# Opening of a transformer kernel: input scale folded into the pool weights, modulation blocks reordered, pool products placed among the running sums

## Chip, core and metric

The kernel runs on one core of a Trainium2 chip. The metric is the device time of one execution in microseconds (us), median of several runs. The engines of the core are named as the profile names them: PE is TensorE (matrix multiply; PEld is its weight load), DVE is VectorE, ACT is ScalarE, POOL is GpSimd, SP is SyncE, which here only issues transfers. All work runs once; each engine has its own instruction stream, and the streams meet at semaphores.

## The reference, cut to the opening

The whole kernel is one pooling layer with a feed-forward part, then two further layers (attention, chunked recurrence, gated spatial mixing). The change touches only the pooling layer, of which this is computed (1024 tokens, 1024 channels, float32):

```
mod = silu(c) @ mod_w + mod_b                      # 6 x 1024 numbers
sh1, sc1, g1, sh2, sc2, g2 = split(mod, 6)
hx = x * (1 + sc1) + sh1
for each group g of 256 channels, window w = 2, 4, 8, 16:
    d = mean of hx over a window of w tokens - hx  # shift cancels in d
    ox = (d @ pool_w[g]) * pool_scale
x = layer_norm(ALPHA * x + g1 * ox, ln_g0, ln_b0)
x = layer_norm(ALPHA * x + g2 * swiglu(x * (1 + sc2) + sh2, ...), ...)
```

## The kernel before

Channels lie on the 128 partitions, so `x` is 8 tiles `resid[:, k, :]` of 128 channels by 1024 tokens, and the layer norm's sums over channels are products with a tile of ones. The layer norm works on two halves of the tokens, `e = 0` and `e = 1`. "Tile 3" or "block 3" below counts from 0.

**Transfers.** SP issues the parameters, the first half of `x`, then the 12 blocks of `mod_w` (2 MB each, three buffers, so a block waits for `mod_mm` of the block three before it), with the second half of `x` ahead of block 2, and then the first weight slabs of the feed-forward part. ACT issues `pw` (the pool weights, 1 MB) and after it `edge` (16 KB, correction factors at the ends of the windows).

**Modulation.** `mod_block(n)` on PE multiplies block n by `silu_c`; `mod_read(n)` on ACT copies the row to `mod_row`; `mod_columns(n)` on PE turns it into 4 columns. Two blocks make one of the six vectors; before, the blocks come in the order shift, scale, gate.

**Pool.** On ACT, `pad(k)` copies tile k into one of three padded buffers `xpad` and `scale_x(k)` multiplies `resid` by ALPHA. On DVE, a running sum over tile k takes 1 to 4 additions (L1814), two small edge corrections (L1823, L1825) and one operation that writes `acc` (L1827). When all 8 are done, DVE forms the scale `sc1p` and `pool_gain` (L1833 to L1838) and passes twice over each tile of `acc` (L1841: scale and add shift; L1842: subtract shift). Then PE computes output tile j from two tiles of `acc` (L812, 4 matmuls), DVE adds it to `resid` (L1868), and PE sums the result for the mean (`mean_part`, L692).

**First norm and projection.** Mean to all partitions (`spread_mean`, L724), subtraction on DVE (`center`, L1877), squares on ACT (L1360), their sums on PE (`square_part`, L692), `root` on ACT (L1364), `reciprocal` on DVE (L1881), `spread_rstd` on PE (L724), then `gain` on DVE (L1888), `tmp` and `h_hi` on ACT (L1427, L1406), and `h_lo` on DVE for even k (L1895), on POOL for odd k (L500). `project_first` (L624 to L626) needs `h_lo` of tile k for its step k, which is 6 matmuls; between the steps of half 0 it sums squares of half 1.

The order on each engine is the order in which the code is written; no scheduler changes it.

Of the kernel before, what the change touches and what calls it, by code (L numbers as in the profile page):

```python
# [24 lines left out]
ALU = mybir.AluOpType  # L25
# [3 lines left out]
P = 128  # L29
# [107 lines left out]
def build(nc, x_t, params, mod_w, pool_w, w_in, w_c, edges, w_spatial, b_spatial, out):  # L137
    with ExitStack() as ctx:
# [73 lines left out]
        MOD_HALF = MOD_BLOCKS // 2  # L212
# [90 lines left out]
        mod_bank = BANK[6]  # L303

# [16 lines left out]
        par_ld, small_ld = beat("par_ld", 16), beat("small_ld", 32)  # L321
# [60 lines left out]
        def _(sp):  # L382
# [11 lines left out]
            for n in range(MOD_BLOCKS):  # L394
                if n >= MOD_BUFFERS:
                    sp.wait_ge(mod_mm.sem, mod_mm.at(n - MOD_BUFFERS))
                if n in X_BEFORE:
                    half = X_BEFORE.index(n)
                    tiles = slice(half * KT // 2, (half + 1) * KT // 2)
                    sp.dma_start(resid[:, tiles, :], x_t[:, tiles, :]).then_inc(x_ld[half].sem, 16)  # L400
                sp.dma_start(mod_big[n % MOD_BUFFERS][:], mod_w[n]).then_inc(mod_ld[n % MOD_BUFFERS].sem, 16)
# [215 lines left out]
        def _(pe):  # L617
# [158 lines left out]
            def mod_columns(n):  # L776

                pe.wait_ge(mod_out.sem, mod_out.at(n))
                for j in range(HALF // P):
                    col = HALF + n * (HALF // P) + j  # L780
                    mm = pe.matmul(PS[1][:, col:col + 1], mod_row[n % 2][:, j * P:(j + 1) * P], ones[:, 0:1], start=True, stop=True,
                                   skip_group_check=True)
                mm.then_inc(mod_turn.sem, 1)

            def mod_part(n):
                mod_block(n)
                if n not in (0, MOD_HALF):
                    mod_columns(n - 1)

            pe.wait_ge(const.sem, 14)  # L790
            pe.wait_ge(siluc.sem, 1)
            pe.wait_ge(dve_first.sem, 1)
            for n in range(MOD_HALF):
                mod_part(n)
            mod_columns(MOD_HALF - 1)

            pe.wait_ge(dve_first.sem, 6)
            pe.matmul(PS[0][:, 0:3], ones[:], lam_prod[:], start=True, stop=True).then_inc(lam_mm.sem, 1)

            pe.wait_ge(small_ld.sem, small_ld.at(0))  # L800
            pe.wait_ge(lam_x.sem, lam_x.at(0))
            pe.wait_ge(mod_col.sem, 1)
            mod_after = {1: 7, 3: 8, 6: 9}
            mod_part(6)
            for j in range(KT):
                g, e = j // 2, j % 2
                pe.wait_ge(p_done.sem, 2 * g + 2)
                if j >= 2:
                    pe.wait_ge(z_done.sem, j - 1)
                for t0 in (0, HALF):  # L810
                    for k in range(2):
                        mm = pe.matmul(pool_bank[e][:, t0:t0 + HALF], pw[:, g, k, e * P:(e + 1) * P],  # L812
                                       acc[:, 2 * g + k, t0:t0 + HALF], start=(k == 0), stop=(k == 1),
                                       skip_group_check=True)
                mm.then_inc(pool_mm.sem, 1)
                if j in mod_after:
                    mod_part(mod_after[j])
                if j >= 1:
                    pe.wait_ge(z_done.sem, j)
                    for half in range(2):  # L820
                        mean_part(0, half, j - 1)

            pe.wait_ge(z_done.sem, KT)
            for e in range(2):
                mean_part(0, e, KT - 1)
# [7 lines left out]
            pe.wait_ge(mod_col.sem, 3)  # L833
# [476 lines left out]
        def _(act):  # L1310
# [27 lines left out]

            act.wait_ge(const.sem, 14)
# [4 lines left out]
            reads = {3: 0, 4: 1, 5: 2, 6: 3, 7: 4}  # L1344
            for k in range(3, KT):
                mod_read(reads[k])
                pad(k)
                scale_x(k)
            mod_read(MOD_HALF - 1)
            act.wait_ge(lam_mm.sem, 1)  # L1350
            act.activation(shift_mean[:], PS[0][:, 2:3], ACT.Identity, scale=1.0 / D, bias=eps[:, 0:1]).then_inc(lam_x.sem, 1)
            act.activation(lam_exp[:], PS[0][:, 0:2], ACT.Exp).then_inc(lam_x.sem, 1)
            for n in range(MOD_HALF, 10):
                mod_read(n)

# [54 lines left out]
            for n in range(KT + 1):  # L1410
                square_centred(0, n)
            mod_read(10)
            root(0, 0)
            for n in range(KT + 1, KT + 4):
                square_centred(0, n)
            mod_read(11)
            act.wait_ge(mod_col.sem, 3)
            for n in range(2 * KT):
                e, k = divmod(n, KT)
                if n in (1, 2, 3, 4):  # L1420
                    square_centred(0, KT + 3 + n)
# [356 lines left out]
        def _(dve):  # L1778
# [24 lines left out]
            dve.wait_ge(small_ld.sem, 32)  # L1803
            for k in range(KT):
# [25 lines left out]
            dve.wait_ge(p_diff.sem, p_diff.at(KT - 1))  # L1830
            dve.wait_ge(mod_turn.sem, mod_turn.at(MOD_HALF - 1))
            nb = COL["mod_b"]
            dve.tensor_tensor(mod[:, 0:24], PS[1][:, HALF:HALF + 24], par[:, nb:nb + 24], ALU.add).then_inc(mod_col.sem, 1)  # L1833
            dve.wait_ge(mod_col.sem, 1)
            dve.tensor_scalar(sc1p[:], mod[:, SC1], 1.0, None, ALU.add).then_inc(px_step.sem, 1)
            step[0] += 1
            dve.wait_ge(px_step.sem, step[0])
            chained(dve.tensor_tensor(pool_gain[:], mod[:, G1], par[:, COL["pool_scale"]:COL["pool_scale"] + KT], ALU.mult))  # L1838

            for k in range(KT):  # L1840
# [3 lines left out]
            def modulation_part(first, blocks):  # L1844

                dve.wait_ge(mod_turn.sem, mod_turn.at(blocks - 1))
                cols, columns = slice(first, 4 * blocks), slice(HALF + first, HALF + 4 * blocks)
                dve.tensor_tensor(mod[:, cols], PS[1][:, columns], par[:, nb + first:nb + 4 * blocks], ALU.add).then_inc(mod_col.sem, 1)

            def modulation_rest():  # L1850

                modulation_part(24, 10)
                dve.wait_ge(mod_col.sem, 2)
                chained(dve.tensor_scalar(sc2p[:], mod[:, SC2], 1.0, None, ALU.add))
                chained(dve.tensor_tensor(ffn_b0[:], ln_b0, sc2p[:], ALU.mult))
                dve.tensor_tensor(ffn_b0[:], ffn_b0[:], mod[:, SH2], ALU.add).then_inc(mod_col.sem, 1)


            ln_b0 = par[:, COL["ln_b0"]:COL["ln_b0"] + KT]
            chained(dve.tensor_scalar(res_b0[:], ln_b0, ALPHA, None, ALU.mult))  # L1860
            chained(dve.tensor_scalar(da_gain[:], par_col("da_g"), 1.0 - LAM_INIT, None, ALU.mult))
            dve.wait_ge(lam_x.sem, lam_x.at(0))
            chained(dve.scalar_tensor_tensor(neg_lam[:], lam_exp[:, 1:2], LAM_INIT, lam_exp[:, 0:1], ALU.subtract, ALU.subtract))

            for j in range(KT):
# [3 lines left out]
                   .then_inc(z_done.sem, 1)  # L1869

# [29 lines left out]
            for n in range(KT, KT + 2):  # L1900
                center(0, n)
            modulation_rest()
            reciprocal(0, 0)
            for n in range(KT + 2, 2 * KT):
                center(0, n)
            for e in range(2):
                for k in range(KT):
                    gain(0, resid, k, e, "ln_g0", n_out)
                    if k % 2 == 1:
                        split_low(0, e * KT + k - 1)  # L1910
                if e == 0:
                    reciprocal(0, 1)
                    modulation_part(40, MOD_BLOCKS)
# [620 lines left out]
```

## Time and profile before

| | |
|---|---|
| median of 3 runs | 3077.92 us (3076.68 to 3078.0) |
| profiled execution, its own time | 3076.16 us |
| its span | 3074.4 us |
| PE busy | 2864.0 us (93%) |
| DVE, ACT, POOL busy | 1453.5, 774.6, 1212.1 us |
| mean granted TensorE clock | 0.97 |

Busy time says how much of the span an engine had an instruction at work. PE is the engine that is busy nearly throughout, so a wait of PE costs time wherever it lies, but the table does not say in which stage it waits; the rows below are of the first 143 us. In the page's line of 40 slices (each 77 us) the first slice of PE has the digit 5, the second 8, nearly all others 9.

### The profile page before, as it was taken

The numbers are of one execution on the slowest core, as the hardware profiler recorded it, in microseconds if no ns is written. First come the engines' busy times: TensorE is split into PE (matmuls) and PEld (weight loads), VectorE is DVE, ScalarE is ACT, GpSimd is POOL, SyncE is SP. The second block draws the span as 40 slices with busy tenths as digits, with TensorE's granted clock in tenths as the row PEclk, the third lists the DMA queues.
The fourth block names the chain that finished last, engine by engine and source line by source line (L and its number), as shares of the span: only waits on it lengthen the run. The fifth ranks groups of instructions, "written<-read, shape, count | busy, mean of one in ns | idle before, by whom it ended". The sixth has DMA issues, their size and how long they took to land.

```text
span 3074.4 us, 38842 instructions
## 1 busy us (share of the span) xinstructions
PE 2864.0 (93%) x14522; PEld 2285.2 (74%) x14522; DVE 1453.5 (47%) x2224; ACT 774.6 (25%) x1383; POOL 1212.1 (39%) x573
## 2 busy tenths in 40 slices
PE   5899999999988899999978998898879999999997
PEld 2578888888866677777756787787658878888885
DVE  7433343343374555565555574737350134444445
ACT  3420000000043333333331322222333331211212
POOL 0254444444343322222221333423254356566554
PEclk9999999999999999999998999999889999999999
DMA  9111111111111001011001111111222211111113
GB/s 370 63 55 48 48 48 48 48 48 48 41 49 69 22 29 33 27 34 34 27 28 28 34 50 41 55 34 48 83 96 89 89 69 69 55 55 68 55 62 117
DMA packets 58223, 185.27 MB, mean 60 GB/s; under 512 B 17300, under 2 KB 17428, under 8 KB 55976
## 3 DMA queue, kind: packets, MB, share of 16 engines
q1 hardware_dynamic: 37152, 152.68, 14.6%
q10 hardware_dynamic: 21000, 31.61, 2.9%
q8 instruction: 49, 0.80, 0.1%
q14 instruction: 22, 0.18, 0.0%
HBM read 163.22 MB, written 21.05 MB: 60 GB/s over the span
## 4 chain that ended last, share of the span: by engine, by line
PE 78%; DVE 11%; issue 4%; ACT 4%; POOL 1%; DMA 1%; DVEq 0%; ACTq 0%; POOLq 0%; SPq 0%
PE ps L624 24%; PE ps L626 23%; PE ps L625 23%; PE ps L954 2%; PE ps L761 1%; PE ps L692 1%; PE ps L965 1%; DVE acc L1932 1%; DVE tree L1814 1%; DVE stat L2081 1%; PE ps L812 1%; DVE da_p L2092 1%; DVE ml_t L2216 1%; DVE da_al L2101 1%; ACT ps L1590 1%
## 5 line engine op out<-in xcount | busy, mean ns | idle before, releaser
L484 POOL TENSOR_TENSOR slab_hi<-slab_raw,zero 128x1024 fp32r<-128x1024 f32 x227 | 442.4, 1949 | 1525.7 <-PE ps L626 1434.4
L624 PE MATMUL ps<-h_hi,slab_hi 128*128 128x512 f32 x2512 | 1001.6, 399 | 25.5 <-DVE h_lo L1895 10.9
L625 PE MATMUL ps<-h_lo,slab_hi 128*128 128x512 f32 x2512 | 988.1, 393 | 0.0
L626 PE MATMUL ps<-h_hi,slab_lo 128*128 128x512 f32 x2512 | 988.1, 393 | 0.0
L486 POOL TENSOR_TENSOR slab_lo<-slab_raw,slab_hi 128x1024 fp32r<-128x1024 f32 x227 | 574.2, 2530 | 17.8
L624 PEld LDWEIGHTS ps<-h_hi,slab_hi 128*128 128x128 f32 x2512 | 478.1, 190 | 137.2 <-issue 21.7
L626 PEld LDWEIGHTS ps<-h_hi,slab_lo 128*128 128x128 f32 x2512 | 477.0, 190 | 102.5
L625 PEld LDWEIGHTS ps<-h_lo,slab_hi 128*128 128x128 f32 x2512 | 478.4, 190 | 95.4
L1932 DVE TENSOR_TENSOR acc<-ps,acc 128x512 f32<-128x512 f32 x448 | 294.9, 686 | 57.5 <-PE ps L626 55.1
L1939 DVE TENSOR_TENSOR ffn_p<-ps,ffn_g 128x1024 f32<-128x1024 f32 x22 | 27.0, 1225 | 456.3 <-PE ps L626 449.1
L1930 DVE SCALAR_TENSOR_TENSOR resid<-ps,mod,resid 128x512 f32<-128x512 f32 x320 | 212.8, 742 | 0.0
L624 PE MATMUL ps<-ffn_hi,slab_hi 128*128 128x512 f32 x352 | 139.4, 396 | 1.4 <-issue 1.4
L625 PE MATMUL ps<-ffn_lo,slab_hi 128*128 128x512 f32 x352 | 138.7, 394 | 0.0
L626 PE MATMUL ps<-ffn_hi,slab_lo 128*128 128x512 f32 x352 | 138.7, 394 | 0.0
L1434 ACT ACTIVATE ffn_g<-ps 128x1024 f32<-128x1024 f32 x22 | 22.6, 1028 | 397.9 <-PE ps L626 397.9
L624 PE MATMUL ps<-sg_yh,slab_hi 128*128 128x512 f32 x256 | 103.8, 405 | 5.4 <-DVE acc L1932 3.4
L2101 DVE TENSOR_TENSOR da_al<-ps,da_ah 128x512 fp32r<-128x512 f32 (+2 forms) x96 | 53.2, 554 | 114.8 <-ACT da_ah L1526 114.7
L626 PE MATMUL ps<-sg_yh,slab_lo 128*128 128x512 f32 x256 | 101.0, 395 | 0.0
L625 PE MATMUL ps<-sg_yl,slab_hi 128*128 128x512 f32 x256 | 100.9, 394 | 0.0
L2081 DVE TENSOR_REDUCE stat<-ps 128x1 f32<-128x256 f32 (+7 forms) x128 | 90.8, 751 | 16.4 <-PE ps L954 15.8
L2356 DVE COPY sg_t<-ps 128x1024 f32<-128x1024 f32 x16 | 19.6, 1225 | 159.1 <-PE ps L761 159.0
L2375 DVE SCALAR_TENSOR_TENSOR sg_v<-ps,par,sg_b 128x1024 f32<-128x1024 f32 x16 | 20.5, 1284 | 150.4 <-PE ps L626 150.4
(315 smaller groups left out, 3847.1 us busy)
## 6 DMA issues: line engine op xcount, KB each, us to landing
slab_raw<-w_in SPq DMA_DIRECT2D x168, 512.0 KB, 3.5
mod_big<-mod_w SPq DMA_DIRECT2D x12, 2048.0 KB, 12.9
slab_raw<-w_c SPq DMA_DIRECT2D x43, 512.0 KB, 3.5
res_scr<-resid ACTq DMA_DIRECT2D x4, 2048.0 KB, 7.6
resid<-res_scr ACTq DMA_DIRECT2D x2, 4096.0 KB, 12.9
gv_scr<-sg_t ACTq DMA_DIRECT2D x16, 512.0 KB, 2.6
slab_raw<-gv_scr SPq DMA_DIRECT2D x16, 512.0 KB, 3.5
resid<-x_t SPq DMA_DIRECT2D x2, 2048.0 KB, 16.8
```

What stands on the lines that cost most here:

```text
L484: pool.tensor_tensor(hi, raw[slot][:], zeros, ALU.add).then_inc(hi_done.sem, 1)
L486: pool.tensor_tensor(wlo[slot][:].rearrange("p k f -> p (k f)"), raw[slot][:], hi.bitcast(F32), ALU.subtract).then_inc(done.sem, 1)
L624: pe.matmul(dst, w_h, r_h, start=first, stop=False, skip_group_check=True)
L625: pe.matmul(dst, w_h, r_l, start=False, stop=False, skip_group_check=True)
L626: return pe.matmul(dst, w_l, r_h, start=False, stop=last, skip_group_check=True)
L692: mm = pe.matmul(bank[32 * g:32 * g + 32, :], weights, tile[:, g * P:(g + 1) * P], start=(opens and k == 0), stop=(k == KT - 1), skip_grou ...
L761: mm = pe.transpose(dst[:, b * P:(b + 1) * P], src(b), ident[:])
L954: mm = pe.matmul(score_bank[c][:, t0:t1], q[rows, cols], k[rows, t0:t1], start=(n == 0 and not diagonal), stop=(n == 2), skip_group_check= ...
L1930: ins = dve.scalar_tensor_tensor(to[:, d, cols], src[:, cols], gain[:, d:d + 1], to[:, d, cols], ALU.mult, ALU.add)
L1932: ins = dve.tensor_tensor(to[:, d, cols], src[:, cols], to[:, d, cols], ALU.add)
L2081: dve.tensor_reduce(stat[:, 4 * (i % 2) + c:4 * (i % 2) + c + 1], PS[c][:, 0:n], AX_X, ALU.max, negate=True)\
L2101: dve.tensor_tensor(a_lo[:, slots, :], turn_bank[:, 0:blocks * P].rearrange("p (b q) -> p b q", q=P), a_hi[:, slots, :].bitcast(F32), ALU. ...
```

## The change

1. **Scale folded into the weights.** The two passes over `acc` (16 operations of 128x1024 on DVE) go. ACT multiplies the pool weights by `sc1p` instead (`scale_weights`, 8 operations of 128x256). The shift is not added and subtracted any more; for `sh1` DVE forms `mod[SH1] - mod[SH1]` and adds it to `ffn_b0`.
2. **Order of the modulation blocks** (`MOD_ORDER`): scale, gate, shift. The scale is read out after 2 blocks, the gate after 4, each into PSUM columns of its own.
3. **Interleaving.** DVE: running sums 0 to 3, scale, sums 4 to 6, gate, the additions to `resid` of tiles 0 and 1, sum 7, the other additions. PE: pool products from after block 1 on, blocks 2 to 9 between them, `mean_part` two tiles behind.
4. **Loads.** `edge` is issued first on ACT's queue; `pw` after the parameters have landed.
5. **Norm.** The Sqrt table is loaded by a dummy operation on `warm` before the mean; DVE subtracts the mean from 4 tiles of half 1 before the first `gain` (instead of 8) and from the other 4 between the gains; the last squares of half 1 move from steps 0 to 3 of `project_first` to steps 3 to 6, and `root(0, 1)` on ACT from before `tmp` 6 to before `tmp` 7. The small operations on the lambdas move to the start.

The core of the diff:

```diff
+        MOD_ORDER = (2, 3, 4, 5, 0, 1) + tuple(range(6, 12))
@@ PE
-            pe.wait_ge(mod_col.sem, 1)
-            mod_after = {1: 7, 3: 8, 6: 9}
-            mod_part(6)
-            for j in range(KT):
-                g, e = j // 2, j % 2
+            def pool_tile(j):
+
+                g, e = j // 2, j % 2
                 pe.wait_ge(p_done.sem, 2 * g + 2)
+                pe.wait_ge(p_diff.sem, p_diff.at(2 * g + 1))
                 if j >= 2:
                     pe.wait_ge(z_done.sem, j - 1)
...
+            mod_block(0)
+            mod_block(1)
+            mod_columns(0)
+            mod_columns(1)
+            pe.wait_ge(lam_x.sem, lam_x.at(0))
+            pool_tile(0)
+            mod_block(2)
+            mod_block(3)
+            mod_columns(2)
+            mod_columns(3)
+            pool_tile(1)
+            mod_block(4)
+            for j in range(2, KT):
+                pool_tile(j)
+                pool_means(j - 2)
+                if j < 7:
+                    mod_block(j + 3)
+                if j == 4:
+                    pe.wait_ge(mod_col.sem, 4)
+                if j < 7:
+                    mod_columns(j + 2)
+            pool_means(KT - 2)
+            pool_means(KT - 1)
             mod_columns(9)
...
             def first_squares(k):
-                if k < 4:
-                    square_part(0, 1, 4 + k)
+                if 3 <= k < 7:
+                    square_part(0, 1, 1 + k)
@@ ACT
-            act.dma_start(pw[:], pool_w).then_inc(small_ld.sem, 16)
             act.dma_start(edge[:], edges).then_inc(small_ld.sem, 16)
             act.wait_ge(par_ld.sem, 16)
+            act.dma_start(pw[:], pool_w).then_inc(par_ld.sem, 16)
...
+            def scale_weights(g):
+
+                act.wait_ge(par_ld.sem, 32)
+                act.wait_ge(mod_col.sem, 2)
+                for k in range(2):
+                    act.activation(pw[:, g, k, :], pw[:, g, k, :], ACT.Copy, scale=sc1p[:, 2 * g + k:2 * g + k + 1]).then_inc(p_done.sem, 1)
...
-                if n == 6:
+                if n == 7:
                     root(0, 1)
@@ DVE
-            for k in range(KT):
-                chained(dve.tensor_scalar(acc[:, k, :], acc[:, k, :], sc1p[:, k:k + 1], mod[:, k:k + 1], ALU.mult, ALU.add))
-                dve.tensor_scalar(acc[:, k, :], acc[:, k, :], mod[:, k:k + 1], None, ALU.subtract).then_inc(p_done.sem, 1)
...
+            for k in range(4):
+                window(k)
+            pool_scale()
+            for k in range(4, 7):
+                window(k)
+            pool_gate()
+            for j in range(2):
+                pool_add(j)
+            window(7)
+            for j in range(2, 5):
+                pool_add(j)
...
-            for n in range(KT + 2, 2 * KT):
+            for n in range(KT + 1, KT + 4):
                 center(0, n)
...
+                    if e == 0 and k in (1, 3):
+                        for n in range(2):
+                            center(0, KT + 3 + k + n)
```

On PE before, around the first pool products (L772 is `mod_block`, L781 `mod_columns`, L798 the lambda product, L812 the pool product; names are the program's):

```order
L781 MATMUL ps<-ones_62,mod_row1_94 128x1 [waits mod_out]
L781 MATMUL ps<-ones_62,mod_row1_94 128x1 x3
L798 MATMUL ps<-lam_prod_76,ones_62 128x3 [waits dve_first]
L772 MATMUL ps<-mod_big0_90,silu_c_70 1x512 [waits mod_ld0,mod_col,mod_out,lam_x,small_ld]
L772 MATMUL ps<-mod_big0_90,silu_c_70 1x512 x7
L812 MATMUL ps<-acc_60,pw_102 128x512 [waits p_done]
L812 MATMUL ps<-acc_60,pw_102 128x512 x3
```

And of the changed program, from the first pool product (L795) on:

```order
L795 MATMUL ps<-acc_60,pw_102 128x512 [waits p_diff,p_done,lam_x]
L795 MATMUL ps<-acc_60,pw_102 128x512 x3
L773 MATMUL ps<-mod_big2_92,silu_c_70 1x512 [waits mod_out,mod_ld2]
L773 MATMUL ps<-mod_big2_92,silu_c_70 1x512 x7
L773 MATMUL ps<-mod_big0_90,silu_c_70 1x512 [waits mod_out,mod_ld0]
...
L782 MATMUL ps<-ones_62,mod_row0_93 128x1 [waits mod_out]
...
L782 MATMUL ps<-ones_62,mod_row1_94 128x1 [waits mod_out]
...
L795 MATMUL ps<-acc_60,pw_102 128x512 [waits p_diff,p_done]
...
L773 MATMUL ps<-mod_big1_91,silu_c_70 1x512 [waits mod_out,mod_ld1]
...
L795 MATMUL ps<-acc_60,pw_102 128x512 [waits z_done,p_diff,p_done]
```

The pool products stood behind blocks 0 to 6; now product 0 stands ahead of block 2, and product 2 is the first that waits for DVE's addition (`z_done`).

On DVE before, from the end of running sum 7 to the first addition to `resid`:

```order
L1827 SCALAR_TENSOR_TENSOR acc_60<-tree3_101,xpad1_96 128x1024 [waits px_step]
L1833 TENSOR_TENSOR mod_69<-ps,par_68 128x24 [waits mod_turn,p_diff]
L1835 TENSOR_SCALAR sc1p_71<-mod_69 128x8 [waits mod_col]
L1838 TENSOR_TENSOR pool_gain_73<-mod_69,par_68 128x8 [waits px_step]
L1841 TENSOR_SCALAR acc_60<-acc_60,sc1p_71,mod_69 128x1024 [waits px_step]
L1842 TENSOR_SCALAR acc_60<-acc_60,mod_69 128x1024 [waits px_step]
...
L1868 SCALAR_TENSOR_TENSOR resid_89<-ps,pool_gain_73,resid_89 128x1024 [waits x_scaled,pool_mm,px_step]
```

And of the changed program, from the end of running sum 6 to the end of sum 7 (L1862 writes `acc`, L1898 adds to `resid`):

```order
L1862 SCALAR_TENSOR_TENSOR acc_60<-tree3_101,xpad0_95 128x1024 [waits px_step]
L1870 TENSOR_TENSOR mod_69<-ps,par_68 128x8 [waits mod_turn]
L1883 TENSOR_TENSOR pool_gain_73<-mod_69,par_68 128x8 [waits mod_col]
L1898 SCALAR_TENSOR_TENSOR resid_89<-ps,pool_gain_73,resid_89 128x1024 [waits x_scaled,pool_mm,px_step]
L1898 SCALAR_TENSOR_TENSOR resid_89<-ps,pool_gain_73,resid_89 128x1024 [waits x_scaled,pool_mm]
L1849 TENSOR_TENSOR tree0_98<-xpad1_96 128x1039 [waits p_diff,px]
...
L1862 SCALAR_TENSOR_TENSOR acc_60<-tree3_101,xpad1_96 128x1024 [waits px_step]
```

The two passes over `acc` are gone, and the first two additions stand ahead of the last running sum.

On ACT before, in half 0 of the projection, from `h_hi` 5 to `h_hi` 7 (L1427 is `tmp`, L1406 `h_hi`, L1364 the root of half 1):

```order
L1406 ACTIVATE h_hi_58<-tmp1_115 128x512 [waits s_tmp]
L1364 ACTIVATE std1_111<-ps,eps_67 128x128 [waits n_ssum]
L1427 ACTIVATE tmp2_116<-resid_89,ffn_b0_75,sc2p_72 128x512 [waits s_lo0,n_out]
L1406 ACTIVATE h_hi_58<-tmp2_116 128x512 [waits s_tmp]
L1427 ACTIVATE tmp3_117<-resid_89,ffn_b0_75,sc2p_72 128x512 [waits s_lo1,n_out]
L1406 ACTIVATE h_hi_58<-tmp3_117 128x512 [waits s_tmp]
```

And of the changed program, at the same place (L1455 is `tmp`, L1432 `h_hi`, L1386 a square, L1390 the root):

```order
L1432 ACTIVATE h_hi_58<-tmp1_115 128x512 [waits s_tmp]
L1386 ACTIVATE sq3_107<-resid_89 128x512 [waits n_ssum,n_cent]
L1455 ACTIVATE tmp2_116<-resid_89,ffn_b0_75,sc2p_72 128x512 [waits s_lo0,n_out]
L1432 ACTIVATE h_hi_58<-tmp2_116 128x512 [waits s_tmp]
L1390 ACTIVATE std1_111<-ps,eps_67 128x128 [waits n_ssum]
L1455 ACTIVATE tmp3_117<-resid_89,ffn_b0_75,sc2p_72 128x512 [waits s_lo1,n_out]
```

The last square of half 1 now stands right before `tmp` 6, and the root between `h_hi` 6 and `tmp` 7.

## Rows read from the trace of the kernel before

**Rows 1.** Chain that ended last, 0 to 143 us: start, us, what.

```profile
1.88 15.81 DMA edge<-edges
...
31.86 1.25 DVE tree L1814
...
49.76 1.25 DVE tree L1814
...
56.50 0.19 DVE mod L1833
...
69.81 1.29 DVE resid L1868
...
79.63 1.83 PE ps L772 x16
81.46 0.98 PE ps L781 x8
82.44 0.57 PE ps L692 x16
83.02 3.63 PE ps L812 x8
...
106.11 5.48 DVE resid L1877 x9
...
112.75 1.28 ACT L1364
114.05 0.38 ACT std L1364
114.45 0.95 DVE rstd L1881
...
134.31 0.81 ACT tmp L1427
...
137.20 0.50 PE ps L624
...
139.78 0.76 DVE resid L1888
```

**Rows 2.** Timeline of PE, opening: start, us, instruction, idle before and releaser.

```profile
21.29 3.59 PE L772 MATMUL ps<-mod_big,silu_c 128*1 128x512 f32 x16 [1.20 <-DMA mod_big<-mod_w]
24.81 1.87 PE L781 MATMUL ps<-ones,mod_row 128*128 128x1 f32 x8
31.08 3.59 PE L772 MATMUL ps<-mod_big,silu_c 128*1 128x512 f32 x16 [4.40 <-DMA mod_big<-mod_w]
...
56.89 3.38 PE L772 MATMUL ps<-mod_big,silu_c 128*1 128x512 f32 x16 [4.63 <-issue]
60.30 7.13 PE L812 MATMUL ps<-acc,pw 128*128 128x512 f32 x16
```

**Rows 3.** Timeline of ACT: first pads, the read of block 0, the root of half 1.

```profile
11.50 2.95 ACT L1332 ACTIVATE xpad<-resid 128x1024 f32<-128x1024 f32 x3 [7.65 <-DMA resid<-x_t]
...
20.15 0.60 ACT L1324 ACTIVATE mod_row<-ps 128x512 f32<-128x512 f32 x1 [2.86 <-PE ps L772]
...
132.67 0.37 ACT L1364 ACTIVATE std<-ps,eps 128x128 f32<-128x128 f32 x1 [2.60 <-PE ps L692]
```

**Rows 4.** Timeline of DVE: the first gain of half 0.

```profile
118.85 1.40 DVE L1888 SCALAR_TENSOR_TENSOR resid<-resid,par,ps 128x512 f32<-128x512 f32 x2
```

**Rows 5.** Timeline of PE: end of the means, and both starts of the projection.

```profile
103.45 0.64 PE L692 MATMUL ps<-resid,ones 128*32 128x128 f32 x16 [0.81 <-DVE resid L1868]
...
122.02 0.76 PE L624 MATMUL ps<-h_hi,slab_hi 128*128 128x512 f32 x1 [3.23 <-DVE h_lo L1895]
...
142.81 0.79 PE L624 MATMUL ps<-h_hi,slab_hi 128*128 128x512 f32 x1 [3.08 <-DVE h_lo L1895]
```

**Rows 6.** Stretch by engine in half 0 of the projection; PEclk is the granted clock.

```profile
122.00:128.50 6.50, 6.48 (x28) 4.00 (x28) 3.20 (x5) 6.37 (x11) 2.57 (x2) 0.52 0.01 3
```

**Rows 7.** Timeline of POOL: the first weight slab is split.

```profile
90.63 1.89 POOL L484 TENSOR_TENSOR slab_hi<-slab_raw,zero 128x1024 fp32r<-128x1024 f32 x1 [85.00 <-DMA slab_raw<-w_in]
```

More of the change, by code:

```diff
@@ L303, in build @@
         mod_bank = BANK[6]
+        mod_cols = [BANK[2][:, QUARTER:QUARTER + 48], BANK[7][:, QUARTER:QUARTER + 48]] + [BANK[3][:, 0:48]] * 4
         res_scr = nc.dram_tensor("res_scr", [P, KT, T], F32, kind="Internal").ap()
@@ L779, in mod_columns @@
                 for j in range(HALF // P):
-                    col = HALF + n * (HALF // P) + j
-                    mm = pe.matmul(PS[1][:, col:col + 1], mod_row[n % 2][:, j * P:(j + 1) * P], ones[:, 0:1], start=True, stop=True,
-                                   skip_group_check=True)
+                    col = MOD_ORDER[n] * (HALF // P) + j
+                    mm = pe.matmul(mod_cols[n // 2][:, col:col + 1], mod_row[n % 2][:, j * P:(j + 1) * P], ones[:, 0:1],
+                                   start=True, stop=True, skip_group_check=True)
                 mm.then_inc(mod_turn.sem, 1)
[L785 to L801, printed above, removed]
-            pe.wait_ge(mod_col.sem, 1)
-            mod_after = {1: 7, 3: 8, 6: 9}
-            mod_part(6)
-            for j in range(KT):
+            def pool_tile(j):
                 g, e = j // 2, j % 2
                 pe.wait_ge(p_done.sem, 2 * g + 2)
+                pe.wait_ge(p_diff.sem, p_diff.at(2 * g + 1))
                 if j >= 2:
@@ L815, in _, with pool_means @@
                 mm.then_inc(pool_mm.sem, 1)
[L816 to L825, printed above, removed]
+            def pool_means(j):
+                pe.wait_ge(z_done.sem, j + 1)
+                for half in range(2):
+                    mean_part(0, half, j)
+            pe.wait_ge(const.sem, 14)
+            pe.wait_ge(siluc.sem, 1)
+            pe.wait_ge(dve_first.sem, 6)
+            pe.matmul(PS[0][:, 0:3], ones[:], lam_prod[:], start=True, stop=True).then_inc(lam_mm.sem, 1)
+            mod_block(0)
[21 more added lines that the diff above has]
+            pool_means(KT - 1)
             mod_columns(9)
@@ L832, in _ @@
             mod_block(11)
-            pe.wait_ge(mod_col.sem, 3)
+            pe.wait_ge(mod_col.sem, 6)
             mod_columns(10)
@@ L1343, in _ @@
                 scale_x(k)
[L1344 to L1347, printed above, removed]
-                scale_x(k)
[L1349 to L1353, printed above, removed]
+            mod_read(0)
+            pad(3)
+            scale_x(3)
+            mod_read(1)
+            pad(4)
+            scale_weights(0)
+            pad(5)
+            for g in range(1, 4):
+                scale_weights(g)
+            pad(6)
+            for k in (4, 5):
+                scale_x(k)
+            mod_read(2)
+            pad(7)
+            scale_x(6)
+            mod_read(3)
+            scale_x(7)
+            for n in range(4, 10):
                 mod_read(n)
+            act.activation(warm[:], eps[:], ACT.Sqrt)
             def square(norm, n, src):
@@ L1836, in _, with modulation_part @@
[L1836 to L1840, printed above, removed]
-                chained(dve.tensor_scalar(acc[:, k, :], acc[:, k, :], sc1p[:, k:k + 1], mod[:, k:k + 1], ALU.mult, ALU.add))
-                dve.tensor_scalar(acc[:, k, :], acc[:, k, :], mod[:, k:k + 1], None, ALU.subtract).then_inc(p_done.sem, 1)
[L1844 to L1848, printed above, removed]
+            def modulation_part(turned, cols):
+                dve.wait_ge(mod_turn.sem, mod_turn.at(turned))
+                dve.tensor_tensor(mod[:, cols], mod_cols[turned // 2][:, cols], par[:, nb + cols.start:nb + cols.stop], ALU.add)\
+                   .then_inc(mod_col.sem, 1)
@@ L1853, in modulation_rest @@
-                dve.wait_ge(mod_col.sem, 2)
+                modulation_part(9, slice(SH2.start, SC2.stop))
+                dve.wait_ge(mod_col.sem, 5)
                 chained(dve.tensor_scalar(sc2p[:], mod[:, SC2], 1.0, None, ALU.add))
                 chained(dve.tensor_tensor(ffn_b0[:], ln_b0, sc2p[:], ALU.mult))
+                chained(dve.tensor_tensor(ffn_b0[:], ffn_b0[:], mod[:, SH1], ALU.add))
                 dve.tensor_tensor(ffn_b0[:], ffn_b0[:], mod[:, SH2], ALU.add).then_inc(mod_col.sem, 1)
-            ln_b0 = par[:, COL["ln_b0"]:COL["ln_b0"] + KT]
@@ L1860, in _, with pool_add @@
[L1860 to L1865, printed above, removed]
+            def pool_add(j):
                 dve.wait_ge(pool_mm.sem, j + 1)
@@ L1869, in _ @@
                    .then_inc(z_done.sem, 1)
+            for k in range(4):
[9 more added lines that the diff above has]
+                pool_add(j)
+            modulation_part(5, SH1)
+            dve.wait_ge(mod_col.sem, 4)
+            chained(dve.tensor_tensor(mod[:, SH1], mod[:, SH1], mod[:, SH1], ALU.subtract))
+            for j in range(5, KT):
+                pool_add(j)
             def center(norm, n):
@@ L1899, in _ @@
                 center(0, n)
-            for n in range(KT, KT + 2):
-                center(0, n)
             modulation_rest()
+            center(0, KT)
             reciprocal(0, 0)
-            for n in range(KT + 2, 2 * KT):
+            for n in range(KT + 1, KT + 4):
                 center(0, n)
```

44 lines of the change are left out of this document (28 added, 16 removed).

## Prediction

> **What bounds the kernel now.** I read the page first: PE is busy for 93% of the span, but only for about half of the first slice. So any time to be had or lost lies where PE waits, and the change lies wholly in the first 143 us. Next I followed the chain that ended last through that stretch [rows 1]. It begins with a transfer: DVE waits for `edge` until 17.7 us, though the first half of `x` was there at 11.50 [rows 3]. From there the chain is DVE alone, running sums until 56.5, small operations, then sixteen passes over `acc`, and at 69.81 the first addition to `resid`. Then it is PE, in a fixed rhythm: product 3.63 us, mean sums 0.57, and three times a modulation block (1.83) with its columns (0.98) [rows 1]. The means end at 103.45 + 0.64 = 104.09 [rows 5]. Then norm: subtraction from 106.11, table load and root, reciprocal, first gain at 118.85 [rows 4], first projection matmul at 122.02 [rows 5]. The reader is to see two engines taking turns: DVE runs while PE has almost nothing (a few blocks between waits for transfers, rows 2), and then PE runs while DVE waits. The change overlaps the turns.
>
> I time it by walking through the changed order with durations of the rows, in the clock of the profiled execution, up to the second projection half (gain 8, before at 139.78). Behind it order and work are the same on all engines, so a shift there goes to the end.
>
> **Up to the scale.** The modulation blocks come by the same transfers, so block 1 still runs at 21.29 and its columns follow. Columns 0 stood at 24.81 for 1.87 [rows 2]; the changed order puts columns 1 directly behind: 28.5 at that pace. DVE's sums 0 to 3 take 31.86 - 17.7 = 14.2 us [rows 1], so they are done by then if they start before 14.3. With `edge` ahead of `pw`, they start when `x` and its pads are there: 11.50 + 1 at the latest, though sum 3 needs `pad(3)`, which stands behind the read of block 0 (20.15, rows 3): 21.8 + 4.3 = 26.1. So the scale waits for PE, and is formed at 28.5 + 0.45 = 28.95. The folding costs ACT eight operations of 128x256. No row has that shape; 128x128 takes 0.37 and 128x512 0.60 [rows 3], and I take 0.4. Only the first two lie on a path (product 0 starts at 29.7); the others, 2.4 us, lie beside DVE's sums 4 to 6.
>
> **The anchor.** DVE goes on with sums 4 to 6. Sum 7 began at 49.76, so they take 49.76 - 31.86 = 17.9 [rows 1]: 46.85. Gate 0.4, one addition 1.3: 48.6. PE meanwhile does product 0, blocks 2 and 3 with their reads on ACT and their columns, product 1 and block 4. At the full clock that ends near 46, and if product 0 runs at half clock (3.3 us more) near 48.5. Product 2 waits for the first addition either way: 48.65. This is where PE stops waiting.
>
> **PE's run.** From there PE has, by the order, products 2 to 7, means 0 to 5, blocks 5 to 9 and columns 4 to 8 without a wait for anything late: 6 x 3.63 + 6 x 0.57 + 5 x 1.83 + 5 x 0.98 = 21.8 + 3.4 + 9.15 + 4.9 = 39.3, so 87.9. Each product needs an addition two back. DVE returns from sum 7 at about 56.5 (48.6 + 1.3 + 6.7), and product 4, the first to need that, comes at 62.7. Means 6 and 7 and the last addition: 89.35. Before it was 104.09, so the gain here is **14.75 us**. The transfers do not stop this: block 11 may be issued when block 8 is done, at 76, before at 81.9, so the weight slabs come no later than the 90.63 of [rows 7]; with four operations of about 2 us on POOL both are split by 99, and they are needed at 105.
>
> **Norm.** The subtraction starts at 91.35. Eight tiles at 0.61 (5.48 over 9, rows 1), five small operations (1.0) and one tile: 97.8. The root no longer has the table load of 1.28 in front [rows 1]; it follows the last of the squares at 97.9, and the reciprocal is done at 99.2. Now another wait ends last: PE still has block 11 and columns 10 ahead of the spread, 97.85 + 1.83 + 0.98 + 1.09 = 101.75. That is gain 0, against 118.85: the gain grows to **17.1**.
>
> **Given back.** Half 0 of the projection. Before, from gain 0 to gain 8 went 139.78 - 118.85 = 20.93. Now the square of the last tile is summed after step 6, and ACT's root stands ahead of `tmp` 7, so step 7 waits for step 6 through the root. Measured from gain 0: `h_lo` 6 is ready at 15.0 (pairs of tiles every 4.1 us while DVE puts subtractions between, then ACT's 1.9 us for each tile with a square), step 6 and the square end at 17.6, root 0.37, and from `tmp` 7 to the matmuls of step 7 took 137.20 - 134.31 = 2.89 [rows 1]. Step 7 starts at 20.85, behind an idle PE of 3.1 us. Before both starts of the projection PE had been idle for 3.08 and 3.23 us [rows 5], and the granted clock behind the latter was 0.52, which is 1.2 GHz [rows 6]; the same after 4.40 and 4.63 us [rows 2], where a block takes 3.59 or 3.38 instead of 1.83. So I take the lower level for step 7 (2.85, as from 122.02 to the second step) and the spread behind it (1.8): gain 8 at 25.5, and **4.6 us** of the 17.1 go.
>
> On this the Trainium skill ("TensorE: Matmul & The Clock Gate", Part 1, What's actually happening) says that the activity window runs freely, not in step with the kernel, so that the same gap may or may not lower the clock. By the row gaps of this size always did; by the page the outcome is open, and then the sum would be that of rival 1.
>
> **Sum.** 17.1 - 4.6 = 12.5. 3076.16 - 12.5 = 3063.7 for an execution like the profiled one; the median of the runs lay 1.8 above it, so **3065.4**.
>
> **Rivals.**
> 1. *Clock stays up across the 3.1 us gap* (chance 0.22). Step 7 takes 1.4 and the spread 0.9: gain 8 at 23.2, gain 14.8, **3063.1**. For it: 3.1 is at the edge of the gaps seen; against it: 3.08 lowered it too [rows 5].
> 2. *The scale is late* (0.10). If `edge` lands no earlier than before, the sums 0 to 3 end at 31.86 and everything up to the anchor is 3.3 later: **3068.7**. Against it: the 16 KB now go first in their queue. Nearby: the interleaved run has waits the sum does not have (an addition late for product 4, which has 62.7 - 57.8 = 5 us of slack).
> 3. *The gain is taken back later* (0.05): some later stage is bound by something that does not move, **3077**. Against it: behind gain 8 no row is bound by a transfer that was issued early; POOL's slabs have about 6 us of slack.
> 4. *Slower: PE runs the interleaved stretch at 1.2 GHz* (0.04). Products are now mixed with blocks whose one-column weights use PE little, and PE idles between 28.5 and 29.7 and perhaps before 48.65. Every us of the 39.3 at the lower level costs one more. The gain is gone once 12.5 of 39.3 run so; all of it is 3065.4 + 39 = **3104**. Against it: before, the same mix ran at 3.63 and 1.83 through 40 us [rows 1], and even the first two products behind a 4.63 us gap took 7.13 together, full pace [rows 2].
>
> **The numbers.** What is left, 0.59, goes to the forecast. Its own bounds: columns 1 at full clock (-0.9), product and block times as they are, the 128x256 operations between 0.2 and 0.6 (only two count, 0.4 each way), the projection at lower clock for longer or shorter (1.5 each way). That gives 3063 to 3068; with rivals 1 and 2 the range is **3061.5 to 3069.5**. A difference of 0.2% is 6.2 us, about what a measurement of this kernel can tell from none. Faster by more: forecast, rivals 1 and 2 except a small part, 0.90; within: 0.06; slower: 0.04.
>
> **What would show it.** In the changed profile: DVE's first running sum at 10 to 13 us instead of 17.7; no waits of DVE in sums 4 to 6; product 2 on PE at 48.65 released by DVE; no idle of PE from there to about 88; means done at 89 to 90; gain 0 near 101.8, released by PE's spread and not by the root; PE idle 3 us before step 7 of the projection; gain 8 at about 127.3 where it was at 139.78. The prediction would be wrong first if product 2 starts past 52, next if blocks take 3.4 instead of 1.8 in the interleaved run, and last if PE's wait before step 7 is not there (then the time is nearer 3061) or is much longer.

## The result and the profile after

The changed kernel takes 3058.54 us (median of 4 runs, 3055.9 to 3059.09) against 3077.3 us before (4 runs, 3075.4 to 3078.0). The ratio is 0.9938 with a 95% interval of 0.9921 to 0.9956, so it is faster by 0.4 to 0.8%. The forecast had the direction, but 12.5 us of gain where 18.8 were measured; the time lies 3 us under the stated range. The profiled spans differ by 3074.4 - 3056.8 = 17.6 us. A second comparison of the same program (`after_again` below) gave 0.995 (0.9936 to 0.9964), a gain of some 15 us by the ratio and 18.6 by the medians (3057.41 against 3076.01). So the runs place the gain at 15 to 19 us, and the two intervals reach from 11 to 24.

The timeline of PE after, from block 0 to the end of the means (start, us, instruction, idle before and releaser); it answers to [rows 2] and the first of [rows 5]:

```profile
15.97 3.59 PE L773 MATMUL ps<-mod_big,silu_c 128*1 128x512 f32 x16 [9.70 <-DMA mod_big<-mod_w]
20.94 3.59 PE L773 MATMUL ps<-mod_big,silu_c 128*1 128x512 f32 x16 [1.38 <-DMA mod_big<-mod_w]
24.46 2.24 PE L782 MATMUL ps<-ones,mod_row 128*128 128x1 f32 x16
28.21 5.37 PE L795 MATMUL ps<-acc,pw 128*128 128x512 f32 x8 [1.51 <-issue]
...
43.46 1.90 PE L773 MATMUL ps<-mod_big,silu_c 128*1 128x512 f32 x16
46.56 3.67 PE L795 MATMUL ps<-acc,pw 128*128 128x512 f32 x8 [1.20 <-DVE resid L1898]
...
53.37 3.68 PE L795 MATMUL ps<-acc,pw 128*128 128x512 f32 x8
...
85.68 0.64 PE L693 MATMUL ps<-resid,ones 128*32 128x128 f32 x16 [0.37 <-DVE resid L1898]
```

Product 2 (46.56) is the last one that DVE releases late. From there to the last mean PE has no wait longer than 0.37 us, and the means end at 86.32 instead of 104.09. The rhythm is 53.37 - 46.56 = 6.81 us for a product, the mean sums of a tile, a block and its columns.

DVE after, its sums and their waits, which answers to the first rows of [rows 1]:

```profile
10.48 1.24 DVE L1849 TENSOR_TENSOR tree<-xpad 128x1039 f32<-128x1039 f32 x1 [2.15 <-DMA edge<-edges]
...
21.21 1.24 DVE L1849 TENSOR_TENSOR tree<-xpad 128x1039 f32<-128x1039 f32 x1 [0.96 <-ACT xpad L1339]
...
26.74 0.17 DVE L1870 TENSOR_TENSOR mod<-ps,par 128x8 f32<-128x8 f32 x1 [1.36 <-PE ps L782]
...
27.02 1.24 DVE L1849 TENSOR_TENSOR tree<-xpad 128x1039 f32<-128x1039 f32 x1
...
45.13 2.48 DVE L1898 SCALAR_TENSOR_TENSOR resid<-ps,pool_gain,resid 128x1024 f32<-128x1024 f32 x2
...
98.34 1.41 DVE L1935 SCALAR_TENSOR_TENSOR resid<-resid,par,ps 128x512 f32<-128x512 f32 x2 [0.58 <-PE ps L725]
...
122.87 1.41 DVE L1935 SCALAR_TENSOR_TENSOR resid<-resid,par,ps 128x512 f32<-128x512 f32 x2 [5.30 <-PE ps L725]
```

The sums start at 10.48 instead of 17.7. The scale (26.74) waits for PE's columns. The first gain (98.34, before 118.85) is released by PE's spread, not by the root. Gain 8, the first of half 1, stands at 122.87, before at 139.78: 16.9 us of the 17.6 are there.

Half 0 of the projection ends with the wait that the change brought in. PE and ACT after:

```profile
119.32 0.50 PE L625 MATMUL ps<-h_hi,slab_hi 128*128 128x512 f32 x1 [3.19 <-POOL h_lo L501]
...
120.92 1.91 PE L725 MATMUL ps<-rstd,ident 128*128 128x128 f32 x8
125.91 0.80 PE L625 MATMUL ps<-h_hi,slab_hi 128*128 128x512 f32 x1 [3.08 <-DVE h_lo L1942]
```

```profile
116.20 0.37 ACT L1390 ACTIVATE std<-ps,eps 128x128 f32<-128x128 f32 x1 [3.58 <-PE ps L693]
```

Step 7 starts behind 3.19 us of idle PE. The root on ACT had waited 3.58 us for the square summed behind step 6, with `tmp` 7 queued behind it. The spread of the reciprocal then takes 1.91 us at a granted clock of 0.50; before, it was this row:

```profile
138.69 1.05 PE L724 MATMUL ps<-rstd,ident 128*128 128x128 f32 x8
```

### The profile page after: what moved, and what is told of

Read it like the earlier page. It is cut to its first block, busy times and chain, and to the rows that moved or that the text cites. A ratio compares the mean times of both kernels' runs of the same rounds, so it can differ in the third digit from the quotient of the medians.

```text
span 3056.8 us, 38843 instructions
## 1 busy us (share of the span) xinstructions
PE 2856.2 (93%) x14522; PEld 2283.4 (75%) x14522; DVE 1442.6 (47%) x2212; ACT 777.6 (25%) x1392; POOL 1212.0 (40%) x573
## 4 chain that ended last, share of the span: by engine, by line
PE 79%; DVE 10%; issue 4%; ACT 4%; DMA 1%; POOL 1%; DVEq 0%; ACTq 0%; SPq 0%; POOLq 0%
PE ps L625 24%; PE ps L627 23%; PE ps L626 23%; PE ps L961 2%; PE ps L762 1%; PE ps L693 1%; PE ps L972 1%; DVE acc L1981 1%; DVE stat L2130 1%; PE ps L795 1%; DMA mod_big<-mod_w 1%; DVE da_p L2141 1%; DVE ml_t L2265 1%; DVE da_al L2150 1%; PE ps L725 1%
## 5 line engine op out<-in xcount | busy, mean ns | idle before, releaser
L2130 DVE TENSOR_REDUCE stat<-ps 128x1 f32<-128x256 f32 (+7 forms) x128 | 90.8, 750 | 17.6 <-PE ps L961 16.9
```

What stands on the lines that cost most here:

```text
L2130: dve.tensor_reduce(stat[:, 4 * (i % 2) + c:4 * (i % 2) + c + 1], PS[c][:, 0:n], AX_X, ALU.max, negate=True)\
```

## Experiments

I used positions in the trace as the main measure (product 2, gain 0, gain 8), since they repeat within 0.5 us for the same order, while whole runs of one program spread by up to 9 us. In each expectation, theory T is what I believed, and a rival is what else the time could have come from. A ratio is the time of the run against the kernel before, with its 95% interval.

**The kernel before with the new load order alone.**

```diff
-            act.dma_start(pw[:], pool_w).then_inc(small_ld.sem, 16)
             act.dma_start(edge[:], edges).then_inc(small_ld.sem, 16)
             act.wait_ge(par_ld.sem, 16)
+            act.dma_start(pw[:], pool_w).then_inc(par_ld.sem, 16)
```

> The kernel before with only the order of the two small loads changed (edge issued first on ACT's queue, pw after the parameters). Theory T (each part alone finds the next wait behind it): DVE starts its sums at 10.5 us instead of 17.7, but pads 3 to 7 on ACT still stand behind the reads of blocks 0 to 4, so the sums end at about 55.3 instead of 56.5: 1 us less, 3076. Rival (parts add up, the early start is worth its own 7.2 us): 3070.

Measured: ratio 0.9996 (0.9987 to 1.0006), with medians of 3075.23 and 3075.51 us. DVE starts at 10.44, and loses the lead in front of the pads. Its timeline, the sums that wait:

```profile
10.44 1.24 DVE L1814 TENSOR_TENSOR tree<-xpad 128x1039 f32<-128x1039 f32 x1 [7.19 <-DMA edge<-edges]
...
21.90 1.24 DVE L1814 TENSOR_TENSOR tree<-xpad 128x1039 f32<-128x1039 f32 x1 [1.69 <-ACT xpad L1332]
...
27.44 1.24 DVE L1814 TENSOR_TENSOR tree<-xpad 128x1039 f32<-128x1039 f32 x1 [1.37 <-ACT xpad L1332]
...
36.51 1.24 DVE L1814 TENSOR_TENSOR tree<-xpad 128x1039 f32<-128x1039 f32 x1 [3.63 <-ACT xpad L1332]
```

Of 7.3 us at the start, 0.9 are left at the first pass over `acc` (56.24 instead of 57.13) and at the means (103.20 instead of 104.09). So far theory T holds. But gain 0 comes at 119.14 and gain 8 at 140.03, both 0.3 later than before: the spread of the mean took 3.39 us instead of 2.03 in this profile, which the last section takes up.

**The kernel before with the fold alone.** The passes over `acc` are left out (with them the adding and subtracting of the shift) and ACT scales `pw` ahead of the read of block 6.

```diff
-                chained(dve.tensor_scalar(acc[:, k, :], acc[:, k, :], sc1p[:, k:k + 1], mod[:, k:k + 1], ALU.mult, ALU.add))
-                dve.tensor_scalar(acc[:, k, :], acc[:, k, :], mod[:, k:k + 1], None, ALU.subtract).then_inc(p_done.sem, 1)
...
+            for g in range(4):
+                for k in range(2):
+                    act.activation(pw[:, g, k, :], pw[:, g, k, :], ACT.Copy, scale=sc1p[:, 2 * g + k:2 * g + k + 1]).then_inc(p_done.sem, 1)
```

> The kernel before with only the fold: ACT scales the pool weights, DVE's sixteen passes over acc are left out, the shift is neither added nor subtracted, all orders as before. Theory T: PE has block 6 until 60.3 us ahead of the first product, so the products start where they did, and only the 0.9 us that PE waited for the first addition goes: 3076.4. Rival (the passes are on the chain that ended last, 12.2 us of it, and come off the time): about 3065.

Measured: ratio 0.9996 (0.9987 to 1.0006), with medians of 3072.11 and 3075.51 us; first product at 60.00 (before 60.30), means done at 102.81 (before 104.09), gain 0 at 118.76 (before 118.85). Taking 12 us of DVE off the chain that ended last moves the means by 1.3 us, and most of that was lost again in a slow spread of the mean:

```profile
56.90 3.17 PE L772 MATMUL ps<-mod_big,silu_c 128*1 128x512 f32 x16 [5.01 <-issue]
...
103.66 3.56 PE L724 MATMUL ps<-mean,ident 128*128 128x128 f32 x16
```

Block 6 stands ahead of the first product and waits for `mod_col`, which DVE gives only when all running sums are done. It starts at 56.90, where it started before (56.89). So the order on PE held the products, and the passes ran beside block 6 and the first two products. The rival's 3065 did not come.

**Both together, old order.**

> The kernel before with the fold and the order of the two small loads together, all other orders as before. Theory T (only the new order on PE and DVE lets the parts count): the means still end near 102 us instead of 104.1, and the time is within 3 us of before, 3073 to 3076. Rival (fold and early start together are the gain, and the order is incidental): 10 us or more less, below 3066.

Measured: ratio 0.999 (0.9981 to 0.9999), 3071.03 us; the means end at 103.36, gain 0 is at 118.12 and gain 8 at 138.58. The position says 1.2 us less than before, the ratio about 3. Either is far from the rival's 10. Here the spread of the mean took 2.03 us, so nothing was lost to the clock there. Theory T's own figure for the means, 102, was 1.4 too early.

**The changed kernel with the old load order.**

```diff
+            act.dma_start(pw[:], pool_w).then_inc(small_ld.sem, 16)
             act.dma_start(edge[:], edges).then_inc(small_ld.sem, 16)
             act.wait_ge(par_ld.sem, 16)
-            act.dma_start(pw[:], pool_w).then_inc(par_ld.sem, 16)
```

> The changed kernel with pw issued ahead of edge again, as before. Theory T: sums 0 to 3 end at 31.9 us instead of 25.4, the scale is formed at 32.2 instead of 26.9, product 2 on PE starts 5.1 us later (51.7 instead of 46.56) and the time is 5 us more than the changed kernel: 3063.6. Rival (my prediction's price of a late scale): 3.3 us more, and a third (early start hidden by something else): no change.

Measured: 3066.05 us, ratio to before 0.9972 (0.9963 to 0.9982). The sums begin at 18.43, product 2 stands at 52.21 (5.65 later) and gain 8 at 129.62 (6.75 later). The load order that is worth next to nothing alone is worth over 5 us in the new order. T had the mechanism; its 5.1 was low, since the sums began 0.7 later than before the change, and step 7 now ran at the lower clock (its first matmul 0.80 instead of 0.50), which makes up the 1.1 between product 2 and gain 8. The rival's 3.3 was too low.

**The changed kernel with running sum 7 first.**

```diff
-            for k in range(4, 7):
+            for k in range(4, 8):
                 window(k)
             pool_gate()
             for j in range(2):
                 pool_add(j)
-            window(7)
```

> The changed kernel with running sum 7 on DVE ahead of the gate and of the first two additions. Theory T: product 2 waits for the first addition, so it starts 6.6 us later, 53.2 instead of 46.56, and behind an idle PE of some 8 us it and the next work start at 1.2 GHz: 6.6 to 10 us more than the changed kernel, 3065 to 3068.5. Rival (PE's run is bound by its own work, and an addition more or less makes no difference): 3058.5.

Measured: 3067.52 us, ratio 0.998 (0.997 to 0.9989), so 9 us of the gain are gone by the medians. PE at product 2 and the next columns:

```profile
53.54 6.00 PE L795 MATMUL ps<-acc,pw 128*128 128x512 f32 x8 [8.48 <-DVE resid L1898]
...
61.76 1.05 PE L782 MATMUL ps<-ones,mod_row 128*128 128x1 f32 x8
```

Product 2 is 7.0 us later, behind 8.48 us of idle PE, and takes 6.00 instead of 3.67. Gain 8 is 9.4 later (132.27). So the place of the first addition on DVE sets the start of PE's run.

**The changed kernel without the early table load.**

```diff
-            act.activation(warm[:], eps[:], ACT.Sqrt)
```

> The changed kernel without the dummy Sqrt, so that the table is loaded in front of the first root, as before. Theory T: PE's block 11 and columns 10 stand ahead of the spread and hide all but 0.2 us: gain 0 at 98.5 us instead of 98.34. Rival (the load's 1.28 us is on the path): gain 0 at 99.6. By the Trainium skill (ScalarE: Activation LUTs, What ACT_TABLE_LOAD costs) a switch costs 2.66 us with its drain; by that, gain 0 would come at about 99.9.

Measured: 3057.74 us, ratio 0.9942 (0.9926 to 0.9957). Gain 0 is at 98.38, as T said, within 0.04 of the changed kernel. The load of 1.28 us is hidden behind PE's block 11. The reciprocal is 0.7 later, and with it the subtractions behind it, so step 7 of the projection starts 0.34 later (119.66). Gain 8 is 0.95 later (123.82); the rest of that is the clock, since the first matmul of step 7 took 0.70 instead of 0.50. The drain that the Trainium skill (ScalarE: Activation LUTs, What ACT_TABLE_LOAD costs) adds does not show here: the load starts at 94.08 and the root at 95.38, 0.02 us behind its end, and gain 0 did not come at 99.9.

**The changed kernel with all subtractions ahead of the gains.**

```diff
-            for n in range(KT + 1, KT + 4):
+            for n in range(KT + 1, 2 * KT):
                 center(0, n)
...
-                    if e == 0 and k in (1, 3):
-                        for n in range(2):
-                            center(0, KT + 3 + k + n)
```

> The changed kernel with all subtractions of the mean in half 1 ahead of the first gain, as before, instead of four of them between the gains. Theory T: the first gain no longer waits for PE's spread (98.34 us) but for DVE, 100.2, but the gains then follow each other every 2.9 us instead of 4.1, and step 6 and the root come no later: gain 8 within 1 us of 122.87 and the time within 1.5 us of the changed kernel. So the 2.7 us that moved between subtraction and first gain are worth nothing by themselves. Rival (they are a gain of their own): 2 us more than the changed kernel.

Measured: 3059.14 us, ratio 0.995 (0.9936 to 0.9963), the same ratio as `after_again`. Gain 0 at 100.06, gain 8 at 124.15, which is 1.3 after the first profile of the changed kernel and 0.8 after the second. Step 7 starts at 119.96, only 0.6 to 0.7 later than in those two. So of the 1.7 us that gain 0 lost, about 1.1 came back; behind it the clock level differs from profile to profile. T's bound of 1 us is missed against the first profile and kept against the second.

**The root one place later.** The root of half 1 is moved from ahead of `tmp` 7 to behind `h_hi` 7.

```diff
-                if n == 7:
+                if n == 8:
                     root(0, 1)
```

> The changed kernel with the root of half 1 on ACT one place later, behind h_hi 7 instead of ahead of tmp 7. Theory T: what the change gave back in half 0 of the projection is this one instruction, which waits for the square summed behind step 6 and holds tmp 7. With it later, step 7 follows step 6 with no idle PE (3.19 us in the changed kernel), the spread behind it stays at 2.4 GHz, and gain 8 comes at about 118.7 us instead of 122.87: 4 us less, 3054.4. Rival (step 7 waits for the low parts on POOL, which are late anyway): gain 8 within 1 us of 122.87.

Measured: 3052.48 us, ratio 0.9926 (0.9912 to 0.994). PE and DVE behind step 7:

```profile
117.53 1.16 PE L725 MATMUL ps<-rstd,ident 128*128 128x128 f32 x8
```

```profile
118.72 1.41 DVE L1935 SCALAR_TENSOR_TENSOR resid<-resid,par,ps 128x512 f32<-128x512 f32 x2 [1.23 <-PE ps L725]
```

Gain 8 is at 118.72, where T put it at 118.7. The idle PE ahead of step 7 is gone, and the spread is back near full pace. The wait that the change brought in is this one instruction's place.

**The late root, and matmuls that fill PE's gaps.** Their result is read by nobody.

```diff
+            def keep_busy(count):
+                for _ in range(count):
+                    pe.matmul(mod_bank[:, 0:P], ident[:], ones[:], start=True, stop=True, skip_group_check=True)
...
             project_first(0, ...)
+            keep_busy(14)
```

A `keep_busy(10)` stands behind the spread of half 1 as well.

> As a_root_last, and with 10 matmuls of 128x128 on PE whose result nobody reads behind the spread of half 1, and 14 behind the projection's first slabs, where PE is idle 3.1 and 3.8 us. Theory T (TensorE falls to 1.2 GHz behind such a gap, and what follows pays): with PE kept at work, both starts run at 2.4 GHz; about 14 matmuls of 128x512 at 0.43 instead of 0.23 us each come off at each place: 3 to 5 us less than a_root_last. Rival (the slow matmuls there are slow for want of operands, not by the clock): the same time as a_root_last.

Measured: 3051.97 us, ratio 0.9921 (0.9907 to 0.9935). Stretches by engine (us, busy and count of PE, PEld, DVE, ACT, POOL; granted clock, DMA share, GB/s), first with the late root alone:

```profile
122.00:126.00 4.00, 4.00 (x10) 3.17 (x11) 3.04 (x5) 3.84 (x6) 1.96 (x2) 0.50 0.00 0
...
140.00:145.00 5.00, 5.00 (x15) 3.91 (x14) 0.00 (x0) 5.00 (x6) 4.92 (x3) 0.56 0.39 118
```

then with the filling matmuls:

```profile
122.00:126.00 4.00, 3.62 (x15) 2.68 (x16) 3.12 (x5) 3.84 (x6) 1.74 (x2) 1.00 0.01 4
...
140.00:145.00 5.00, 5.00 (x24) 4.14 (x23) 0.00 (x0) 5.00 (x6) 5.00 (x3) 1.00 0.47 180
```

The granted clock is 1.00 instead of 0.50 (1.2 GHz), and 15 and 24 matmuls start where 10 and 15 did. So it was the clock and not the operands. Half 1 ends only 1.2 us earlier (POOL's next slab split at 133.74 instead of 134.92), as its steps now wait for low parts. The next stage adds to it: the split that stood at 152.93 stands at 149.39, and the 3.54 us are still there at the gate of the feed-forward part (ACT at 710.08 instead of 713.62). That is within T's 3 to 5 us. The medians differ by 0.5 us only, and their intervals overlap, so the times do not confirm it.

**Repeats on one chip.** Three programs were run once more side by side.

> The changed kernel once more, so that its clock can be seen in a second profile and the next two can be set against it on one chip. My prediction took 1.2 GHz for step 7 of the projection and for columns 0 and 1. Theory T (the level behind a gap of about 3 us is open, the rest repeats): product 2 at 46.5 us, gain 0 at 98.3, both within 0.3, and gain 8 between 122.2 and 123.9. Rival (columns and step 7 ran faster by a chance of that execution, and the whole opening moves): product 2 at 48.

> The kernel with the root of half 1 one place later, again, beside the changed kernel on the same chip. Theory T: gain 8 at 118.7 us and 4 us less than the changed kernel, ratio to before 0.9925. Rival (the first comparison came from different chips): no difference to the changed kernel.

> The kernel with the late root and the 24 filling matmuls, again. Theory T: the granted clock stays 1.00 from 116 to 150 us, but steps 8 to 15 then wait for low parts, so only 1 to 3 us come off against the late root alone: ratio to before 0.992. Rival: equal to the late root alone.

Measured: 3057.41 us and 0.995 (0.9936 to 0.9964) for the changed kernel, 3057.77 and 0.994 (0.9926 to 0.9953) with the late root, 3055.09 and 0.9928 (0.9914 to 0.9941) with the filling as well. Gain 8 is at 123.34, 118.80 and 119.18. For the changed kernel T held (gain 0 at 98.29). PE in the second profile of the changed kernel:

```profile
20.99 1.90 PE L773 MATMUL ps<-mod_big,silu_c 128*1 128x512 f32 x16 [1.35 <-DMA mod_big<-mod_w]
22.82 1.95 PE L782 MATMUL ps<-ones,mod_row 128*128 128x1 f32 x16
...
46.50 3.67 PE L795 MATMUL ps<-acc,pw 128*128 128x512 f32 x8 [0.27 <-DVE resid L1898]
...
119.24 0.80 PE L625 MATMUL ps<-h_hi,slab_hi 128*128 128x512 f32 x1 [3.19 <-POOL h_lo L501]
...
121.97 1.33 PE L725 MATMUL ps<-rstd,ident 128*128 128x128 f32 x8
```

Block 1 took 1.90 us here and 3.59 in the first profile of the same program, behind nearly the same wait (1.35 and 1.38 us). Product 2 came at 46.50 and 46.56. So the level of the clock early on differs from run to run, and the overlap hides it. Step 7 behind the same 3.19 us ran at the lower clock here (0.80, and 0.50 in the first profile), and the spread mostly at the higher (1.33, and 1.91). In times, the late root is not shown to be faster on this chip: the medians are equal, the intervals overlap, and the forecast 4 us (ratio 0.9925) did not come. That it is the faster one rests on gain 8 in the traces, 4.2 and 4.5 us earlier, and on both its ratios being lower. For the filling, the slab split behind the next stage came 1.5 us earlier (149.60 against 151.13) and half 1 itself no earlier (133.97 against 133.88), which is within T's 1 to 3 us, and the granted clock was 1.00 from 116 to 150 us as T said. With the 3.5 of the first pair this fits a worth that depends on how long the clock stays low without it: with the late root alone, the slow matmuls from 139 us on lasted to 144.2 in the first profile and to 141.6 in the repeat. The version with both has the lowest median in both sets of runs, with overlapping intervals.

## Why the prediction was right in kind and short in size

The time came 6.9 us under the forecast of 3065.4. Four terms of the sum make 4.4 of that, and the largest is the start of PE's run.

- *Where the gain is.* Right: the two turns of DVE and PE overlap, and PE's run starts at product 2, released by the first addition. Moving that addition took 9 us away.
- *Up to the scale.* This is the step that failed most. I placed columns 0 and 1 one behind the other at 1.87 us each, to 28.5, and the scale at 28.95. They took 2.24 together in one profile and 1.95 in the other, and sum 4 began at 27.02 instead of 28.95. Even with PE done by 24.8 (`after_again`), product 2 was at 46.50: the second half of `x` and its pad then set the start of sum 4. This second bound was in no term of mine. The term was 1.9 us too high. From the start of sum 4 to product 2 it took 19.5 instead of 19.7 us, together 2.1. The trace of before had a row with the columns of two blocks together, behind a block that was slow too (3.24 us), and I did not use it:

```profile
50.09 1.95 PE L781 MATMUL ps<-ones,mod_row 128*128 128x1 f32 x16
```

- *PE's run.* I added spacings of the old chain (3.63, 0.57, 1.83, 0.98, together 7.01); in the new order they are 3.61, 0.46, 1.83 and 0.92, together 6.81. PE waits in neither (it is busy throughout 75.36 to 82.37 before and 50.16 to 56.98 after), and the clock is 1.00 in both. What differs is which operation follows which; why that costs 0.2 us, no run here shows. It makes 0.9 by the last mean.
- *Norm.* 0.4 more by gain 0: 98.34 instead of 101.75. I let block 11 start 6.5 us after the subtraction, behind five small operations of DVE and a ninth tile. The squares of half 0 wait for neither, and block 11 started 6.07 after it (94.42).
- *Given back.* The mechanism was exact: step 7 began 20.98 us after gain 0, forecast 20.85, behind 3.19 us of idle PE. But of the two things priced at 1.2 GHz only the spread ran so. Step 7's six matmuls ran at full pace in the first profile, all but the end of the last. The cost was 3.6, not 4.6, which is the 1.0 that is left. In the second profile of the same program, behind the same 3.19 us, step 7 was slow and the spread mostly fast. My rule that such a gap always lowers the clock at once was wrong. On this the Trainium skill ("TensorE: Matmul & The Clock Gate", Part 1, What's actually happening) had left the outcome open, and the two profiles agree with it.
- *Sum.* 2.1 + 0.9 + 0.4 + 1.0 = 4.4, which with 12.5 is the 16.9 measured at gain 8. Behind it come 0.4 up to the next slab split (17.3) and 0.3 to the end. The last 1.8 of the 6.9 are the distance from the profiled execution to the median, which I carried over from the runs before. After the change the median lay 0.07 below the profiled execution. That distance is a matter of a few runs and not of the kernel: its coming out at nothing was luck, and without it the forecast would still have been 5 us too high.
- *Rivals.* The clock across the 3.1 us gap (rival 1) came out between rival and forecast: step 7 as the rival had it, the spread as I had it. The late scale (priced 3.3) costs 5.7 at product 2 and 6.75 at gain 8 when tried; its price was counted from my 28.95, which was too late. The gain was not taken back later. The slower clock in PE's run did not occur: in every profile of the changed order all products from 2 on took 3.67 or 3.68, but for the one behind 8.48 us of idle PE.
- *The range* did not hold the time. All terms leaned the same way, and of the 2.1, 0.9 and 0.4 the range allowed for 0.9 only, a faster pace of columns 1.

## What to carry to other kernels

Taking an operation off the chain that ended last is worth only the distance to the next wait: 12 us of DVE work and 7 us of a late load were worth about 1 us each alone. The load counted (6.75 us at gain 8) once the order on both engines let it. What the fold is worth in the new order was not tried. When an instruction that waits (here a root) stands in a queue, ask what stands behind it; moving it one place brought the next stage 4 us forward. A spacing belongs to a pair of neighbours: the same four operations took 7.01 us in one order and 6.81 in another, with no wait in either. And before taking a duration from a row at the low clock, look for others of the same shape: here one at full pace was in the trace.

## What was unexpected of the hardware

The granted clock fell in PE's work without any long gap: with the fold alone, the spread of the mean took 3.56 us instead of 2.03, and the granted clock was 0.77 from 105 to 110 us, though PE was busy for 4.97 of these 5 us and had been idle for no more than 0.80 ahead of it. With the new loads alone it took 3.39 (granted clock 0.71 in the same stretch, PE busy for all of it), and with both together 2.03. In the second profile of the changed kernel the clock fell to 0.52 from 102.4 to 105.6 us, in half 0 of the projection, behind an idle PE of 1.23 us; in the first profile it stayed at 1.00 there behind 1.24. So the lower level is not tied to an idle PE of 3 us alone. What decides it, these runs do not show.
